# Experts' products as three fp16 products of high and low parts, with the experts' weights split during the projection stage

## The chip, the cores and the metric

One Trainium2 chip, one of its cores. The metric is the device time of one execution in microseconds (us), lower is better. TensorE, VectorE (DVE), ScalarE (ACT), GpSimd (POOL) and SyncE (SP) each work through their own instructions in order and wait for one another on semaphores. DMAs are issued from SP's, ScalarE's and GpSimd's queues.

## The reference

One layer of a streaming encoder over 4096 prompt tokens and 8 streams of 16 new tokens (33 tiles of 128 tokens), all in fp32:

```python
proj = rmsnorm(x) @ w_in                          # 1024 -> 3080 columns
out_a = rglru(causal_conv(x_lru)) * gelu(y_lru)   # a recurrence over time
o = gdn_sequence(q, k, v, g, beta)                # gated delta rule, chunks of 64 tokens
x = x + concatenate([out_a, norm(o) * silu(z)]) @ w_out
h = rmsnorm(x)
grp = argmax(h @ rg_w + rg_b)                     # 1 group of 4
top2 of the 8 experts of that group               # 32 experts in all
y = (silu(xblk @ w1[e]) * (xblk @ w3[e])) @ w2[e] # blocks of 128 tokens of one expert, 1024 -> 256 -> 1024
x = x + w_0 * y_0 + w_1 * y_1
return rmsnorm(x), states
```

## The kernel before, in words

Five stages follow one another, each a block with one program per engine.

**Projection** (`project_phase`). Nine groups of tokens: eight of 512 (`groups`, 0 to 7) and one of 128 (`stream=True`). A group is normed, transposed by TensorE (L279, T0 to T7, into four PSUM banks `turned`), and split into a high half `h_hi` by ScalarE (L355) and a low half `h_lo` by VectorE (L474), both fp16. Then 24 chunks of 128 output columns follow in the order of `sequence()`: Y and X (recurrence), Q (delta rule's q, k, v), Z (its gate). Each is 24 products of 512 columns in fp16: `w_hi h_hi`, `w_hi h_lo`, `w_lo h_hi` for eight slices of the inner width (L292). Three PSUM banks `pP` take turns; ScalarE empties them (L369, L376, L407), VectorE convolves the X and Q chunks (L496 to L505). G is the recurrence's gates (TensorE L301, ScalarE L382 to L386), R and O the recurrence and its store, S the silu of a convolved chunk (L400) and its store, N the squares for the next group's norm (L340) and the scaling of its rows, B the two small logits of the delta rule. In group 0 the weights `w_in` are loaded chunk by chunk into `stage` (two halves that take turns) and split: ScalarE makes `w_hi` (L348), VectorE `w_lo` (L467), and SP loads the next but one piece when `w_lo` is done (`w_split`, L221).

**Mixing** (`mix_phase`). 33 tiles; three of them are in work at a time, as X, Y and R steps of the list `MIX`, which fixes each engine's order. X builds the triangular inverse of the delta rule through a chain T, W, I, Z over TensorE, ScalarE and VectorE (L844, L854, L866, L1166); Y applies it and multiplies by `w_out`; R norms, routes and stores the normed rows `h2`. For the routing VectorE runs r0 and r1 on small operands; `h2` is made by GpSimd (step h2, L1087) and stored by ScalarE (step sh, L1037). `so` squares `ob` on ScalarE (L1025), `on` scales it on VectorE.

**Routing** (`routing_phase`). VectorE makes the tables of blocks; SP starts the loads of the first two experts.

**Experts** (`experts_phase`). 98 blocks of 128 rows, each of one expert, in the order of `EXPERTS`: `up` of block b+1 (L1539, eight fp32 products of 512 columns), `gT` of block b (L1547, two transposes), T0 and T1 of block b+2 (L1529, eight transposes), d0 and d1 of block b (L1557, four fp32 products of 512 columns). ScalarE does silu, gTc (copies the gated rows out of PSUM, L1578), T0c and d0c; VectorE does mul (L1606), T1c and d1c. GpSimd gathers the rows of a block. SP loads the weights of expert e+2 (3 MB, two DMAs, L1343) when the last block of expert e is done; `up` of the first block of e+2 waits for them (`ready`, which SP raises at L1489).

**Combine** (`combine_phase`). Gathers both experts' rows for each tile, adds, norms and stores.

What sets the order of the work around the change: `sequence()`, `MIX` and `EXPERTS`, and in the experts' stage the counts of blocks per expert.

## Time and profile before

| | us |
|---|---|
| median of 3 runs | 4444.15 |
| lowest and highest | 4443.91, 4451.27 |
| span of the profiled execution | 4435.0 |
| busy in it: TensorE, VectorE, ScalarE, GpSimd | 3787.8, 1902.0, 1410.0, 831.1 |

The profile is of one execution of the kernel. Its page gives busy time per engine, the span in 40 equal slices (a digit is the busy share in tenths; for the clock, tenths of full speed, and 9 is 90% or more), and the chain of work that ended last. That chain covers only the last 20 us here, so stages are read from stretches of the span and from the waits. In a line of the trace, "L292 MATMUL pP<-h_lo,w_hi" is a product of source line 292 that writes tile pP; "[1.93 <-SPq L1489]" says that the engine stood idle 1.93 us before it and that SP's queue at line 1489 released it. "x16" is a run of 16 such instructions, shown as one.

### The profile page before, as it was taken

What the parts mean: (1) busy time and instruction counts of PE and PEld (TensorE: products, weight loads), DVE (VectorE), ACT (ScalarE), POOL (GpSimd) and SP (SyncE); (2) the same over time, 40 slices, a digit from 0 to 9 for tenths busy, and PEclk for the clock granted to TensorE, in tenths of its full rate; (3) what the DMA queues carried; (4) which work ended last, traced back from release to release, by engine and by line L of the source; (5) the groups of instructions that cost most, each with busy time, mean ns of one, the idle gap of its engine ahead of it and who ended that gap; (6) DMA issues with size and microseconds to landing.
All of it is one profiled execution on the core that took longest, in us unless ns stands there. A gap on an engine that the chain in (4) does not pass through costs nothing. (4 is left out here: it accounts for less than half of the span.)

```text
span 4435.0 us, 64350 instructions
## 1 busy us (share of the span) xinstructions
PE 3787.8 (85%) x19068; PEld 2250.3 (51%) x19069; DVE 1902.0 (43%) x4556; ACT 1410.0 (32%) x2749; POOL 831.1 (19%) x853
## 2 busy tenths in 40 slices
PE   7999999999869989998988998839999999999600
PEld 3444444444556766666666666624444444444200
DVE  6456544564435565555555556441111111111255
ACT  6445544555423333333333333201111111111111
POOL 0000000000023333333333333201111111111133
PEclk9999999999979999999999999969999999999855
DMA  4211111111132112112111211023455455542387
GB/s 150 83 67 40 50 47 61 47 47 38 39 115 65 62 57 64 53 61 67 54 62 57 64 62 57 32 97 140 177 192 187 180 189 198 197 173 95 131 280 266
DMA packets 221780, 454.93 MB, mean 103 GB/s; under 512 B 20818, under 2 KB 132818, under 8 KB 213074
## 3 DMA queue, kind: packets, MB, share of 16 engines
q1 hardware_dynamic: 138498, 220.96, 14.8%
q10 hardware_dynamic: 54288, 146.56, 8.4%
q0 software_dynamic: 28864, 86.09, 6.0%
q14 instruction: 99, 0.81, 0.1%
q8 instruction: 31, 0.51, 0.0%
HBM read 303.84 MB, written 149.71 MB: 102 GB/s over the span
## 5 line engine op out<-in xcount | busy, mean ns | idle before, releaser
L1539 PE MATMUL ebank<-w,rowsT 128*128 x1568 | 708.0, 605 | 35.8 <-SPq L1489 32.5
L292 PE MATMUL pP<-h_hi,w_hi 128*128 128x512 f16 (+1 forms) x1728 | 623.7, 365 | 32.5 <-DVE h_lo L474 16.9
L292 PE MATMUL pP<-h_lo,w_hi 128*128 128x512 f16 (+1 forms) x1728 | 623.4, 365 | 0.0
L292 PE MATMUL pP<-h_hi,w_lo 128*128 128x512 f16 (+1 forms) x1728 | 623.2, 364 | 0.0
L1539 PEld LDWEIGHTS ebank<-w,rowsT 128*128 128x128 f32 x1568 | 302.8, 194 | 426.8 <-issue 426.8
L1557 PE MATMUL ebank<-w,guT 128*128 x784 | 353.4, 593 | 2.6 <-ACT guT L1578 2.6
L1606 DVE TENSOR_TENSOR gu<-ebank,sil 128x256 f32<-128x256 f32 x98 | 41.6, 425 | 703.8 <-ACT sil L1574 703.8
L505 DVE SCALAR_TENSOR_TENSOR cv<-win,cols_sb,cv 128x512 f32<-128x512 f32 (+1 forms) x432 | 305.3, 707 | 35.1 <-issue 3.6
L1574 ACT ACTIVATE sil<-ebank 128x256 f32<-128x256 f32 x98 | 37.7, 385 | 826.3 <-PE ebank L1539 826.3
L1166 DVE TENSOR_TENSOR WI<-bank,const 128x512 f32<-128x512 f32 x198 | 136.5, 689 | 376.6 <-PE bank L844 372.0
L292 PEld LDWEIGHTS pP<-h_hi,w_hi 128*128 128x128 f16 x1728 | 171.9, 100 | 220.9 <-issue 28.9
L1065 POOL TENSOR_TENSOR B<-G,const 128x512 f32<-128x512 f32 x198 | 256.2, 1313 | 143.7 <-DVE G L1147 138.8
L844 PEld LDWEIGHTS bank<-Tm,B 128*128 128x128 f32 x1584 | 195.0, 194 | 158.8 <-ACT Tm L995 78.5
L935 PE MATMUL bank<-w_out,mx 128*128 128x512 f32 x528 | 269.5, 594 | 0.8 <-DVE mx L1228 0.8
L844 PE MATMUL bank<-Tm,B 128*128 128x128 f32 x1584 | 228.0, 288 | 46.6 <-ACT Tm L991 42.7
L292 PEld LDWEIGHTS pP<-h_lo,w_hi 128*128 128x128 f16 x1728 | 172.0, 100 | 186.2 <-issue 11.2
L292 PEld LDWEIGHTS pP<-h_hi,w_lo 128*128 128x128 f16 x1728 | 172.1, 100 | 181.7 <-issue 0.8
L923 PE MATMUL bank<-w_out,ft 128*128 128x512 f32 x528 | 247.9, 593 | 0.0
L854 PEld LDWEIGHTS bank<-WI,Zm 128*128 128x128 f32 x1320 | 162.1, 193 | 142.9 <-ACT Zm L1003 71.8
L854 PE MATMUL bank<-WI,Zm 128*128 128x128 f32 x1320 | 192.5, 289 | 48.2 <-DVE WI L1166 34.3
L1557 PEld LDWEIGHTS ebank<-w,guT 128*128 128x128 f32 x784 | 140.9, 189 | 143.7 <-issue 143.7
L252 POOL TENSOR_TENSOR ss<-ss,eps 128x4 f32<-128x4 f32 (+1 forms) x9 | 1.8, 198 | 1111.2 <-ACT junk L340 1111.2
(282 smaller groups left out, 5691.6 us busy)
## 6 DMA issues: line engine op xcount, KB each, us to landing
w<-in_w SPq DMA_DIRECT2D x32, 2048.0 KB, 9.1
y<-yb ACTq DMA_DIRECT2D x98, 512.0 KB, 4.8
ft<-mixin SPq DMA_DIRECT2D x33, 1280.0 KB, 6.3
mixin<-qo ACTq DMA_DIRECT2D x128, 256.0 KB, 2.0
w<-in_w SPq DMA_DIRECT2D x32, 1024.0 KB, 12.5
xt<-in_x SPq DMA_DIRECT2D x33, 512.0 KB, 5.9
xr<-in_x SPq DMA_DIRECT2D x33, 512.0 KB, 4.7
x<-x2b ACTq DMA_DIRECT2D x33, 512.0 KB, 4.9
```

The source lines that it names most:

```text
L292: ins = nc.tensor.matmul(pP[n % NPB][:, 0:N], w[:, k, c0:c0 + P], h[:, k, 0:N], start=(k + i == 0), stop=(k == KD - 1 and i == 2))
L505: ins = nc.vector.scalar_tensor_tensor(dst, window(c, j, stream), cw(j), dst, ALU.mult, ALU.add)
L844: ins = nc.tensor.matmul(XB[:, h, :], Bs[s][:, h, :], Tm[:, h, :], start=True, stop=True)
L854: ins = nc.tensor.matmul(XC[:, h, :], Zm[:, h, :], WI[:, h, :], start=True, stop=True)
L923: ins = nc.tensor.matmul(flat((YD, YE)[half]), ft[p][:, QC + ZC + c, :], w_out[:, c, half * 512:half * 512 + 512], start=(c == 0), stop=False)
L935: nc.tensor.matmul(flat((YD, YE)[half]), mx[:, h, :], w_out[:, LC + h, half * 512:half * 512 + 512], start=False, stop=(h == H - 1)).then_ ...
L1065: nc.gpsimd.tensor_tensor(Bs[s][:, :, :], G[:, :, :], heads(mat(f"level{s}")), ALU.mult).then_inc(*did(n))
L1166: nc.vector.tensor_tensor(WI[:, :, :], XB[:, :, :], heads(mat("ident")), ALU.add).then_inc(*did(n))
L1539: ins = nc.tensor.matmul((M0, M1)[p][:, :], xT[p][:, k, :], w13[:, bass.ds(s, 1), k * 512:(k + 1) * 512].rearrange("p a n -> p (a n)"), st ...
L1557: ins = nc.tensor.matmul((OA, OB)[h][:, :], guT[p][:, k, :], w.rearrange("p a n -> p (a n)"), start=(k == 0), stop=(k == FE // P - 1))
L1574: nc.scalar.activation(sil[p][:, :], (M0, M1)[p][:, 0:FE], ACT.Silu).then_inc(*did(n))
L1606: nc.vector.tensor_tensor(gu[p][:, :], (M0, M1)[p][:, FE:2 * FE], sil[p][:, :], ALU.mult).then_inc(*did(n))
```

## The change

- The products `up` and `down` of the experts are each three fp16 products (high x high, high x low, low x high) in place of one fp32 product. The rows `h2` are stored as an fp16 high and low half (2 x 1024 columns, as many bytes as before) and transposed in fp16, 16 transposes in place of 8. The gated rows are split when they leave PSUM: ScalarE makes the high half (gTc), VectorE the low one (new step gTl).
- In the mixing stage ScalarE makes the high half of `h2` (new step hh) and VectorE the low half (new step hl); ScalarE's store (sh) waits for hl. GpSimd scales `ln2_row` once by 16.
- The experts' weights are 192 pieces of 128x1024 fp32. They are split into fp16 halves in groups 1 to 7 of the projection stage, 28 pieces in each of groups 1 to 6 and 24 in group 7: a step W follows each Y, X and Q chunk, two follow each Z chunk. SP loads a piece into `stage`, ScalarE makes its high half, VectorE (one W step later) the low half, and SP stores both to `ws` in HBM. Two buffers take turns. The experts' stage loads `ws` (one DMA an expert, 3 MB as before).
- Of the constant matrices only the identity is loaded in the first stage, the others at the start of the mixing stage.

```diff
-    return out + [("Z", 0), ("S", QC - 1), ("Z", 1), ("Z", 2), ("Z", 3)]
-
-
-def project_phase(nc, T, gb, const, cols):
+    out += [("Z", 0), ("S", QC - 1), ("Z", 1), ("Z", 2), ("Z", 3)]
+    paced, n = [], 0
+    for kind, m in out:
+        paced.append((kind, m))
+        if kind in "YXQZ":
+            for _ in range(2 if kind == "Z" else 1):
+                paced.append(("W", n))
+                n += 1
+    assert n == NW
+    return paced
...
+        halves = sb("halves", [P, 2, 2, WC], FP16)
...
+            def halved(g, j):
+
+                q = (g - 1) * NW + j
+                sp.wait_ge(expert_lo, q + 3)
+                sp.dma_start(T["ws"][bass.ds(q, 1)].rearrange("a p n -> p (a n)"),
+                             halves[:, j % 2, :, :].rearrange("p h n -> p (h n)")).then_inc(halves_out[j % 2], 16)
+
+            def experts(g):
+                n = steps_of(g)
+                for j in range(n):
+                    q = (g - 1) * NW + j
+                    sp.wait_ge(expert_lo, q + 1)
+                    sp.dma_start(stage[:, j % 2, :, :].rearrange("p k n -> p (k n)"),
+                                 T["we"][bass.ds(q, 1)].rearrange("a p n -> p (a n)")).then_inc(expert_in[j % 2], 16)
+                    if j:
+                        halved(g, j - 1)
+                halved(g, n - 1)
+
+            sp.wait_ge(w_split, len(wblocks))
+            with sp.Fori(1, groups - 1) as g:
+                load(g + 1, GT)
+                experts(g)
             load(groups, 1)
+            experts(groups - 1)
...
+                def expert_half(j):
+                    q = (g - 1) * NW + j
+                    act.wait_ge(expert_in[j % 2], ((g - 1) * (NW // 2) + j // 2 + 1) * 16)
+                    act.wait_ge(halves_out[j % 2], ((g - 1) * (NW // 2) + j // 2 + 1) * 16)
+                    nc.scalar.activation(halves[:, j % 2, 0, :], stage[:, j % 2, :, :].rearrange("p k n -> p (k n)"),
+                                         ACT.Copy, scale=W_SCALE).then_inc(expert_hi, 1)
...
+                    elif kind == "W":
+                        if not first and not stream and m < steps_of(g):
+                            expert_half(m)
...
+                def expert_rest(j):
+                    q = (g - 1) * NW + j
+                    dve.wait_ge(expert_hi, q + 1)
+                    nc.vector.scalar_tensor_tensor(halves[:, j % 2, 1, :], stage[:, j % 2, :, :].rearrange("p k n -> p (k n)"),
+                                                   W_SCALE, halves[:, j % 2, 0, :], ALU.mult, ALU.subtract
+                                                   ).then_inc(expert_lo, 1)
+
                 for kind, m in seq:
                     if first and block_of.get((kind, m), len(wblocks)) + 2 < len(wblocks):
                         split(block_of[kind, m] + 2)
                     if kind == "N" and following:
                         norm(g + 1, following)
+                    elif kind == "W":
+                        if not first and not stream and 0 < m <= steps_of(g):
+                            expert_rest(m - 1)
...
+                if not first and not stream and steps_of(g) == NW:
+                    expert_rest(NW - 1)
...
-R.lg.pe Y.so.act Y.ro.pool R.r0.dve R.sh.act
+R.lg.pe R.hh.act Y.so.act Y.ro.pool R.r0.dve R.hl.dve R.sh.act
...
+                elif n == "hh":
+                    act.wait_ge(h2_out, 16 * (t + 1))
+                    act.wait_ge(*at("h2", t))
+                    nc.scalar.activation(h2s[:, 0, :], h2b[:, :], ACT.Copy).then_inc(*did(n))
                 elif n == "sh":
-                    act.wait_ge(*at("h2", t))
-                    act.dma_start(T["h2"][bass.ts(t, P), :], h2b[:, :]).then_inc(h2_out, 16)
+                    act.wait_ge(*at("hl", t))
+                    act.dma_start(T["h2"][bass.ts(t, P), :], h2s[:, :, :].rearrange("p h n -> p (h n)")).then_inc(h2_out, 16)
...
-                    pool.wait_ge(h2_out, 16 * (t + 1))
+                    pool.wait_ge(*at("hl", t, 1))
...
+                elif n == "hl":
+                    dve.wait_ge(*at("hh", t))
+                    nc.vector.tensor_tensor(h2s[:, 1, :], h2b[:, :], h2s[:, 0, :], ALU.subtract).then_inc(*did(n))
...
-O.gT.pe O.gTc.act
+O.gT.pe O.gTc.act O.gTl.dve
...
-    w13, w2, loaded = weights
-    for dst, src in ((w13, "w13"), (w2, "w2")):
-        engine.dma_start(dst[:, p, :], T[src][bass.ds(e, 1)].rearrange("a p n -> p (a n)")).then_inc(loaded[p], 16)
+    ws, loaded = weights
+    engine.dma_start(ws[:, p, :, :], T["ws"][bass.ds(e * EC, EC)].rearrange("c p n -> p c n")).then_inc(loaded[p], 16)
...
-                    for k in range(4):
-                        c = 4 * h + k
-                        ins = nc.tensor.transpose(bank[:, k * P:(k + 1) * P], xb[p][:, c * P:(c + 1) * P], ident)
+                    for k in range(KD):
+                        ins = nc.tensor.transpose(bank[:, k * P:(k + 1) * P], xb[p][:, h, k * P:(k + 1) * P], ident16[:, :])
...
-                        ins = nc.tensor.matmul((M0, M1)[p][:, :], xT[p][:, k, :],
-                                               w13[:, bass.ds(s, 1), k * 512:(k + 1) * 512].rearrange("p a n -> p (a n)"),
-                                               start=(k == 0), stop=(k == KD - 1))
+                        for i, (x, w) in enumerate(PARTS):
+                            ins = nc.tensor.matmul((M0, M1)[p][:, :], xT[p][:, x, k, :], half(s, k // 2, w, k % 2 * 512),
+                                                   start=(k + i == 0), stop=(k == KD - 1 and i == 2))
...
-                    pe.wait_ge(*at("gTc", b))
+                    pe.wait_ge(*at("gTl", b))
                     for k in range(FE // P):
-                        w = w2[:, bass.ds(pe_slot[0], 1), k * D + h * 512:k * D + h * 512 + 512]
-                        ins = nc.tensor.matmul((OA, OB)[h][:, :], guT[p][:, k, :], w.rearrange("p a n -> p (a n)"),
-                                               start=(k == 0), stop=(k == FE // P - 1))
+                        for i, (x, w) in enumerate(PARTS):
+                            ins = nc.tensor.matmul((OA, OB)[h][:, :], guT[p][:, x, k, :],
+                                                   half(pe_slot[0], W13 // WC + k, w, h * 512),
+                                                   start=(k + i == 0), stop=(k == FE // P - 1 and i == 2))
...
+                elif n == "gTl":
+                    dve.wait_ge(*at("d1", b, 2))
+                    dve.wait_ge(*at("gTc", b))
+                    nc.vector.tensor_tensor(guT[p][:, 1, :, :].rearrange("p k n -> p (k n)"), GB[:, 0:FE],
+                                            guT[p][:, 0, :, :].rearrange("p k n -> p (k n)"), ALU.subtract).then_inc(*did(n))
```

## Rows read from the trace of the kernel before

**Rows 1.** Page, 40 slices: TensorE's busy tenths, and its granted clock.

```profile
PE   7999999999869989998988998839999999999600
...
PEclk9999999999979999999999999969999999999855
```

**Rows 2.** Tile xt, three groups: loads by SP, and time to landing.

```profile
L202 SPq DMA_DIRECT2D xt<-in_x x12: 332/333/333, 460.9 to 749.0; - x12
...
DMA to landing us min/median/max: 3.1/5.1/6.6
```

**Rows 3.** Stretches of a group: length, busy us by engine, clock, DMA.

```profile
485.50:530.30 44.80, 43.43 (x190) 19.45 (x188) 30.60 (x52) 36.62 (x44) 0.00 (x0) 1.00 0.06 23
530.30:583.30 53.00, 53.00 (x332) 25.30 (x330) 34.84 (x71) 23.41 (x37) 1.21 (x2) 1.00 0.15 54
583.30:598.00 14.70, 14.70 (x70) 6.69 (x69) 0.00 (x0) 1.84 (x4) 0.00 (x0) 1.00 0.19 71
```

**Rows 4.** One experts block in time: start us, us, engine, line, op.

```profile
3404.99 7.03 PE L1539 MATMUL ebank<-w,rowsT 128*128 x16
...
3411.86 0.38 PE L1547 MATMUL ebank<-const,gu 128*128 128x128 f32 x2
...
3412.08 1.04 PE L1529 MATMUL ebank<-const,rows 128*128 128x128 f32 x8
...
3412.47 0.42 DVE L1606 TENSOR_TENSOR gu<-ebank,sil 128x256 f32<-128x256 f32 x1 [6.59 <-ACT sil L1574]
...
3412.95 3.61 PE L1557 MATMUL ebank<-w,guT 128*128 x8
```

**Rows 5.** Experts: waits (us, times, longest); one load; TensorE behind it.

```profile
PE ebank L1539 <- SPq L1489: 32.5, 15, 2.4
...
3607.81 0.85 SPq L1343 DMA_DIRECT2D w<-in_w  x2
...
3621.01 8.82 PE L1539 MATMUL ebank<-w,rowsT 128*128 x16 [1.99 <-SPq L1489]
```

**Rows 6.** Mixing stage, one tile in time.

```profile
1704.38 0.40 ACT L1025 ACTIVATE junk<-ob,sc 128x128 f32<-128x128 f32 x1 [5.41 <-DVE ob L1221]
...
1710.15 0.68 DVE L1166 TENSOR_TENSOR WI<-bank,const 128x512 f32<-128x512 f32 x1
...
1710.88 1.16 PE L854 MATMUL bank<-WI,Zm 128*128 128x128 f32 x8 [0.51 <-DVE WI L1166]
```

**Rows 7.** Projection, TensorE in time: two products in a row.

```profile
500.06 0.38 PE L292 MATMUL pP<-h_lo,w_hi 128*128 128x512 f16 x1
500.28 0.38 PE L292 MATMUL pP<-h_hi,w_lo 128*128 128x512 f16 x1
```

**Rows 8.** First group in time: a low part, load, high part.

```profile
106.45 1.22 DVE L467 SCALAR_TENSOR_TENSOR w_lo<-stage,w_hi 128x1024 f16<-128x1024 f32 x1
...
107.69 0.54 SPq L221 DMA_DIRECT2D stage<-in_w_in  x1
...
111.98 1.06 ACT L348 ACTIVATE w_hi<-stage 128x1024 f16<-128x1024 f32 x1 [0.45 <-DMA stage<-in_w_in]
```

**Rows 9.** DMA issues: a 512 KB store, median us to landing.

```profile
h<-h2b ACTq DMA_DIRECT2D x33, 512.0 KB, 2.6
```

**Rows 10.** Projection in time: evacuation, silu, convolution, square, B step.

```profile
538.79 0.60 ACT L376 ACTIVATE win<-pP 128x512 f32<-128x512 f32 x1 [2.02 <-PE pP L292]
539.44 0.63 ACT L400 ACTIVATE qo<-cv 128x512 f32<-128x512 f32 x1
...
539.51 0.17 DVE L496 COPY win<-carry 128x3 f32<-128x3 f32 x1
...
540.39 2.40 DVE L505 SCALAR_TENSOR_TENSOR cv<-win,cols_sb,cv 128x512 f32<-128x512 f32 x3
...
551.16 1.06 ACT L340 ACTIVATE junk<-xt 128x1024 f32<-128x1024 f32 x1 [0.90 <-issue]
...
574.78 0.18 DVE L546 SCALAR_TENSOR_TENSOR amax<-asum,alog 128x16 f32<-128x16 f32 x1 [4.86 <-ACT alog L420]
```

More of the change, by code:

```diff
@@ L44 @@
 PROJ = 1.0 / (W_SCALE * H_SCALE)
+G_SCALE = 4.0
+WC = 1024
 W13, W2 = KD * 2 * FE, (FE // P) * D
+DOWN = 1.0 / (W_SCALE * G_SCALE)
+EC = (W13 + W2) // WC
+NW = 28
 COLS = {}
@@ L193, in project_phase @@
         table_out = sem("table_out")
+        expert_in = [sem(f"expert_in{n}") for n in range(2)]
+        expert_hi = sem("expert_hi")
+        expert_lo = sem("expert_lo")
+        halves_out = [sem(f"halves_out{n}") for n in range(2)]
+        NC = NE * EC
+        steps_of = lambda g: NW if not isinstance(g, int) or g < groups - 1 else NC - NW * (groups - 2)
         block = ctx.enter_context(nc.Block())
@@ L221, in _ @@
                 sp.dma_start(stage[:, n % 2, :, 0:w], T["w_in"][:, :, c:c + w]).then_inc(weights_in[n % 2], 16)
-            with sp.Fori(2, groups) as g:
-                load(g, GT)
+            def halved(g, j):
[17 more added lines that the diff above has]
+                experts(g)
             load(groups, 1)
+            experts(groups - 1)
+            for p in range(2):
+                sp.wait_ge(halves_out[p], 16 + NC // 2 * 16)
             sp.wait_ge(zeroed, 1)
@@ L456, in _ @@
                 dve.sem_inc(s, 16)
+            dve.sem_inc(expert_lo, 2)
             def norm(g, nt):
@@ L1487, in arrived @@
             def arrived(e, p):
-                sp.wait_ge(loaded[p], (e - p) * 16 + 32)
+                sp.wait_ge(loaded[p], (e - p) * 8 + 16)
                 sp.sem_inc(ready, 1)
@@ L1544, in step @@
                     pe.wait_ge(*at("gTc", b, 1))
+                    pe.wait_ge(*at("gTl", b, 1))
                     pe.wait_ge(*at("mul", b))
```

76 lines of the change are left out of this document (44 added, 32 removed).

## The prediction

> **What bounds the kernel now.** I read the 40 slices first, then busy times by stage, then the waits, and last single stretches in order of time. The slices show three stages in which TensorE is busy (projection to about 1180 us, mixing to about 2940, experts to about 4170) and a tail without it [rows 1]. In the projection one group of 512 tokens takes 143.2 us (the first loads of x in three groups' views run from 460.9 to 749.0; less the 1.6 us that the four loads of a group are apart, this is two groups), and TensorE is busy in nearly all of it [rows 2, 3]. The reader should see where the others have room: in the stretch with the gates ScalarE is busy 36.6 of 44.8 us, in the next 23.4 of 53.0, and VectorE does nothing in the last 14.7 us of a group [rows 3]. In the experts' stage one block takes 11.40 us and TensorE never pauses inside it; fifteen times it waits some 2.2 us for weights [rows 4, 5]. In the mixing stage TensorE waits once a tile for a chain that passes through VectorE [rows 6].
>
> **Experts' stage.** A block's up products are eight fp32 products of two passes each, 16 in the 6.87 us between 3404.99 and 3411.86, 0.43 each; an fp16 product of 512 columns starts every 0.216 us in the projection [rows 4, 7]. Up: 16 x 0.43 = 6.87 becomes 24 x 0.216 = 5.18. Down: 8 x 0.43 = 3.44 becomes 12 x 0.216 = 2.59. The 8 transposes took 0.87 (3412.08 to 3412.95); 16 in fp16 of 128 columns at a quarter of 0.216 take 0.86. The two of the gated rows stay at 0.22 [rows 4]. Before: 6.87 + 0.22 + 0.87 + 3.44 = 11.40; after: 8.86. A wait is added: the down product now needs a VectorE subtraction (gTl) behind ScalarE's copy. On VectorE it queues behind the product of the next block's gate, which ends at 3412.89; gTl, like that product 0.42, ends at 3413.31 and the down product starts at about 3413.33, where its turn is 3412.95 [rows 4]: 0.38 us, so 9.24 us a block. Behind gTl VectorE queues only the second transposed copy, which has the 2.59 us of the down product as cover. 98 x (11.40 - 9.24) = 212 us gained.
>
> Against this stand the weight loads. They start when the last block of expert e is done and are needed by e+2, so an expert with two blocks covers one block's time. A load issued at 3607.81 let TensorE go at 3621.01, 13.2 us later, and others lie up to 13.7 [rows 5]. Bytes are the same (3 MB), so I keep 13.5: the stall grows from 2.2 to 13.5 - 9.24 = 4.3 us, 15 times: 64 instead of 32.5. Some of these stalls cost more: 16 passes take 8.82 us behind this one and 7.03 undisturbed, 1.8 us more, as behind 10 of the 15 [rows 4, 5]. It is the granted clock, which stands at 9 tenths and more in all slices but those of the stages' joints and the tail, where TensorE has stood [rows 1]; it falls from 2.4 to 1.2 GHz for a while. With 4.3 us idle I count all 15: 27 instead of 18. Together +40. **Stage: -172** (bounds -150, if loads slow to 15 us beside denser traffic, and -190, if gTl is hidden).
>
> **Projection stage: the new ring.** 192 pieces of weight (128x1024) are split in groups 1 to 7, 28 a group (24 in the last). Each costs ScalarE 1.05 us and VectorE 1.22, as the splits of the first group do [rows 8]. As busy time it fits. But the pieces go through two buffers, and each turn is a ring over four queues: VectorE's low part of piece j ends, SP stores j and loads j+2 behind it, ScalarE makes the high part of j+2 (waiting in order, the evacuations of PSUM queued behind), and VectorE makes the low part one slot later, behind the next chunk's convolution. I call D the time from the end of a low part to the start of the high part two pieces on. In the first group, without the store, D is 4.3 us: the low part ends at 107.67, the load goes at 107.69, the high part starts at 111.98 [rows 8]. Here the load's runs are 4 KB: such a load lands in 3.1 us when alone, and the four in a row take 6.4 to 6.6 for the last, issued 1.6 us after the first, so 1.5 apart [rows 2]. The store of 512 KB (a like one lands in 2.6 [rows 9]) is issued 0.54 before. If the load merely follows by issue, D = 0.54 + 3.1 + 0.2 = 3.8; if it also waits for the store's packets, 2.6 + 1.5 + 0.1 = 4.2. I take 4.2, and up to 5.1 where stores of the convolution's output cut in (0.5 MB per two slots).
>
> A Trainium skill rule bears on this D. DMA: Bandwidth & Descriptors, "Two DMAs through the same engine are not ordered", says descriptors of one queue start in order but are pipelined, with reads and writes in separate queues; by it the load needn't wait for the store's writes, D would be 3.8 and the sum below 29 us less. No row here has a store directly before a load on SP's queue.
>
> In the slots of the convolution two slots make one ring: D 4.2 + high 1.05 + silu and its store issue 1.2 + evacuation of the next chunk 0.65 + convolution 3.3 + low 1.22 + hand-overs 0.2 = 11.8 us, where TensorE needs 2 x 24 x 0.216 = 10.36 [rows 7, 8, 10]. In the four Z chunks, with two pieces each, a ring is 4.2 + 1.05 + 1.22 + 0.1 = 6.6 against 5.18. So the ring, not TensorE, sets the pace. I walked one group in queue order with these durations (the same walk gives 145.2 us for the group of before, which took 143.2). From the last transpose on:
> - To the end of Q2's evacuation: 70.0 before, 79.8 after. ScalarE had 8 us idle in the gates' stretch [rows 3] and gets some 9 high parts plus ring waits.
> - To Z0's evacuation: 55.2 before; five rings are 59, and the next group's squares (four of 1.06 with small reads behind them, 4.9 on ScalarE) and the B step, for which VectorE waits 4.9, hold two rings longer [rows 10]: 72.3 after.
> - To the next group's first low half: 17.4 before; four rings of 6.6 less the part already under way: 27.5 after.
>
> TensorE has three PSUM banks, so it runs ahead of ScalarE by at most three chunks, finishes Z3 and then stands some 20 us, because ScalarE turns to the next group's h_hi only behind its last high part. 182.0 - 145.2 = 37 us a group, six groups, and 14 for the last, which has no pieces in its last two chunks: **+235** (D 3.8: +206; D 5.1: +301). After a pause of that length the clock falls as above; 1.7 us a group and little else, since the other pauses are ScalarE's anyway: +13 (0 to +35). **Stage: +248.**
>
> **Mixing stage.** Per tile ScalarE gets hh (1.05) and VectorE hl (1.22, two sources in SBUF, going on from 0.42 at 256 columns and 0.69 at 512, as WI's, by 0.53 for 512 more [rows 4, 6]). hh falls where ScalarE had stood 5.4 us before the squares of ob (1704.38), and h2 is long there: nothing; without that cover it would cost 1.05 a tile. hl stands ahead of r1, on and I2 in VectorE's queue. There VectorE works without a gap until WI at 1710.15, and TensorE waits 0.5 us for it at 1710.88 [rows 6]. So hl goes on the path whole: 33 x 1.22 = **+41** (0 to +60). The store of h2 now waits for hl in ScalarE's queue and holds the first Tm a little; that is covered, since its product meets VectorE's delay anyway. POOL's h2 waits for hl instead of the store: no cost.
>
> **Small edits.** The constant matrices (896 KB, 2.6 us at 1.5 us per 512 KB [rows 2]) are loaded at the mixing stage's start instead of the kernel's, all but one, and POOL scales one row there before it begins. What the start gains the joint loses; for the scaling **+2**, bounds -3 and +8. One DMA in place of two per expert, and the half-width junk: nothing, for they lie behind waits that stay.
>
> **Sum.** -172 + 248 + 41 + 2 = +119. The profiled execution's span is 4435.0, the median 4444.15; the 9.1 us around it stay. 4444 + 119 = **4563 us**.
>
> **Rivals.**
> - *The pieces are hidden.* If D comes out so short or ScalarE so early that the ring stays under 10.36 us, which needs D below 2.8, only their busy time in the gates' stretch is left: the walk gives +4.9 a group, +35. Then 4444 - 172 + 35 + 41 + 2 = 4350, faster. It decides from D = 2.8 down. Against it: even the first group's load alone takes 4.3. For it: by busy time alone there is room on both engines [rows 3].
> - *The ring is slower.* Stores and loads at 1 MB a piece with the output stores beside them push D to 5.1, clock drops cost 30: 301 + 30 + 41 + 2 - 160 = +214, 4658.
> - *The mixing stage takes nothing*, as other waits absorb hl: 4522; inside the forecast's own range.
> - *The fp16 products don't run at 0.216 in this stage*: then the gain shrinks, 4650 or so; nothing supports it but that the loads and gathers are denser.
>
> **How the numbers follow.** Forecast 0.70 (4465 to 4640), hidden pieces 0.14, slower ring or dearer products 0.16. The range is 4465 (D 3.8, mixing 0, experts -190, no clock cost) to 4680 (slower ring): 0.82. About 0.2% (9 us) is what a measurement can tell from no change. Faster 0.14 (the hidden pieces), within 0.2% 0.03 (a ring halfway, D near 3), slower 0.83.
>
> **What would show it.** In the changed profile: groups 1 to 6 about 180 us apart, ScalarE waiting for the DMA into stage, VectorE's h_lo late, and TensorE idle some 20 us before its transposes' second half; mixing tiles 1.2 us longer; blocks of 9.24 us, and fifteen waits of 4 us for weights. Groups of 150 us or less would refute the ring; blocks over 9.5 or a stage over 1010 us the experts' term.

## The result, and the profile after

The changed kernel takes **4858.14 us** (median of 4 runs, 4853.62 to 4866.4) where the kernel before takes 4444.53 (4443.91 to 4451.27): ratio **1.093**, 95% interval 1.0915 to 1.0946. The sign of the forecast was right, the size was not: 4563 us was forecast, and 4858 lies outside its range of 4465 to 4680. The profiled execution's span is 4864.8 us (4435.0 before).

The page of the changed kernel, in 40 slices: TensorE's busy tenths and its granted clock, which answer to [rows 1].

```profile
PE   8878686686867688888888888888489897888600
...
PEclk9989898898988799999999999998699998999855
```

The projection stage now shows sixes and sevens where [rows 1] had nines, and there the clock falls to 8 and 7. The stages' lengths, read from the first and last squares of the mixing stage (tile sqb) and the first and last down products, say where the time went:

| us | before | after | difference | forecast |
|---|---|---|---|---|
| projection, to the first sqb | 1256.6 | 1628.3 | +371.7 | +248 |
| mixing, first to last sqb | 1540.2 | 1679.5 | +139.3 | +41 |
| experts, first to last down product | 1154.9 | 1060.2 | -94.7 | -172 |
| joints and tail | | | +13.5 | +2 |

**Projection.** Loads of x of two groups, five groups apart (start, us, engine, line, tiles), as in [rows 2]:

```profile
173.54 1.96 SPq L221 DMA_DIRECT2D xt<-in_x  x4
...
1172.13 1.98 SPq L221 DMA_DIRECT2D xt<-in_x  x4
```

That is 199.7 us a group ((1172.13 - 173.54) / 5), 143.2 before: six groups make some 336 us of the stage's 372. From the load of x of the 128 tokens (1370.1) to the first sqb it is 258 us, 223 before: 35 more. Two stretches of one group (columns as in [rows 3]):

```profile
690.00:751.00 61.00, 40.69 (x247) 19.03 (x244) 29.66 (x47) 26.68 (x39) 1.21 (x2) 0.83 0.60 207
751.00:772.00 21.00, 3.67 (x16) 3.27 (x16) 9.39 (x11) 9.37 (x13) 0.00 (x0) 0.50 0.63 226
```

In the last 21 us TensorE is busy for 3.7 (at a granted clock of 0.50), VectorE and ScalarE for 9.4 each: nobody is full, all turn round the ring of the pieces. One turn of it (VectorE's low parts, SyncE's stores and loads, ScalarE's high parts, from three answers in order of time by engine):

```profile
1124.81 1.22 DVE L535 SCALAR_TENSOR_TENSOR halves<-stage,halves 128x1024 f16<-128x1024 f32 x1
```

```profile
1126.22 0.35 SPq L246 DMA_DIRECT2D ws<-halves  x1
1126.85 0.33 SPq L254 DMA_DIRECT2D stage<-in_we  x1
```

```profile
1130.86 1.06 ACT L405 ACTIVATE halves<-stage 128x1024 f16<-128x1024 f32 x1 [5.54 <-DMA stage<-in_we]
...
1135.91 1.06 ACT L405 ACTIVATE halves<-stage 128x1024 f16<-128x1024 f32 x1 [2.15 <-DMA stage<-in_we]
```

The low part ends at 1126.03, the high part two pieces on starts at 1130.86: D is 4.8 us, and 5.5 in the next turn (1130.36 to 1135.91). The page's groups of instructions and of DMA issues (KB each, median us to landing) say that this is the rule:

```profile
L405 ACT ACTIVATE halves<-stage 128x1024 f16<-128x1024 f32 x192 | 202.5, 1055 | 486.8 <-DMA stage<-in_we 485.3
...
stage<-in_we SPq DMA_DIRECT2D x192, 512.0 KB, 4.6
ws<-halves SPq DMA_DIRECT2D x192, 512.0 KB, 3.0
```

ScalarE waits 485 us for loads of pieces. The median load lands in 4.6 us; 3.1 is the fastest of the twelve loads of x in [rows 2], on which D was built. From the low part's end: 0.19 to the store, 0.63 to the load, 4.6 to its landing, 0.1 to ScalarE: D is 5.5. Taken piece by piece from the trace, its median is 5.5 too, and its mean higher (6.7), since ScalarE comes late to some pieces between two groups.

**Waits of TensorE** (us in total, times, longest). L1577 answers to L1489 of [rows 5]; the last line, idle time put down to no engine, has no counterpart there.

```profile
PE pT L322 <- DVE h_lo L528: 177.9, 9, 28.5
PE bank L924 <- DVE WI L1242: 113.4, 32, 3.7
...
PE ebank L1625 <- SPq L1577: 63.3, 15, 4.7
...
PE ebank L1625 <- issue: 44.8, 81, 0.8
```

**Mixing.** The chain of [rows 6] in a tile of the changed kernel, VectorE first, then GpSimd and TensorE:

```profile
2215.30 1.22 DVE L1325 TENSOR_TENSOR h2s<-h2b,h2s 128x1024 f16<-128x1024 f32 x1
...
2218.06 2.78 DVE L1347 SCALAR_TENSOR_TENSOR esel<-lg,goh,esel 128x8 f32<-128x8 f32 x3
...
2222.05 1.76 DVE L1301 TENSOR_TENSOR onb<-ob,ro 128x512 f32<-128x512 f32 x1
2223.73 0.68 DVE L1242 TENSOR_TENSOR WI<-bank,const 128x512 f32<-128x512 f32 x1
```

```profile
2218.33 1.27 POOL L1139 TENSOR_TENSOR B<-G,const 128x512 f32<-128x512 f32 x1
2219.55 1.26 POOL L1133 TENSOR_TENSOR AT<-AT,const 128x512 f32<-128x512 f32 x1
2220.78 5.37 POOL L1139 TENSOR_TENSOR B<-G,const 128x512 f32<-128x512 f32 x4
```

```profile
2224.46 1.75 PE L924 MATMUL bank<-WI,Zm 128*128 128x128 f32 x8 [3.66 <-DVE WI L1242]
2226.01 3.00 PE L993 MATMUL bank<-w_out,ft 128*128 128x512 f32 x4
```

hl takes the 1.22 us forecast. But the three products on esel, 8 columns wide, take 2.78 us together; before they took 0.86. They now lie beside GpSimd's products, and onb takes 1.76. WI, one of whose inputs is in PSUM, lies beside them too and takes the 0.68 of [rows 6]. TensorE waits 3.66 us, not 0.51, and then eight products take 1.75 instead of the 1.16 of [rows 6], since the granted clock is lower: over the two runs of products above it is 0.62 of full speed in the mean (its two levels are 1.2 and 2.4 GHz), and it was 1.00 over the same two runs of the kernel before (columns as in [rows 3]):

```profile
2224.46:2229.01 4.55, 4.55 (x14) 2.86 (x15) 0.00 (x0) 0.60 (x1) 1.69 (x2) 0.62 0.00 0
```

```profile
1710.88:1713.76 2.88, 2.88 (x14) 1.88 (x15) 0.00 (x0) 0.60 (x1) 2.88 (x4) 1.00 0.00 0
```

The kernel before already had such a meeting, of an instruction one column wide with GpSimd's mask (the like one takes 0.15 us in the changed kernel, at 2221.98):

```profile
1708.39 1.24 DVE L1276 TENSOR_TENSOR dif<-m8e 128x1 f32<-128x1 f32 x1
1709.55 0.68 DVE L1225 TENSOR_TENSOR onb<-ob,ro 128x512 f32<-128x512 f32 x1
```

```profile
1708.29 1.31 POOL L1065 TENSOR_TENSOR B<-G,const 128x512 f32<-128x512 f32 x1
```

**Experts.** One block, as in [rows 4]:

```profile
3618.97 5.35 PE L1625 MATMUL ebank<-ws_sb,rowsT 128*128 x24 [0.39 <-issue]
...
3624.37 1.06 PE L1614 MATMUL tbank<-ident,rows 128*128 128x128 f16 x16
3625.69 2.76 PE L1643 MATMUL ebank<-ws_sb,guT 128*128 x12 [0.26 <-DVE guT L1699]
3629.18 1.03 PE L1625 MATMUL ebank<-ws_sb,rowsT 128*128 x4 [0.73 <-issue]
```

The up product's 24 passes take 5.35 with the last one's end, as summed. From the first transpose to the down product it is 1.32 us, the low part's wait of 0.26 in it, where 0.86 + 0.38 = 1.24 were forecast. New is the idle time before `up`, 0.39 and 0.73 us in turns, put down to no engine. Ahead of it the end of the last pass shows as well: twelve passes that start 0.216 apart end after 2.76 us, not 2.59. A block takes 10.05 us (the second `up` behind this one starts at 3639.06, two blocks on), not 9.24.

### The profile page after: what moved, and what is told of

The parts are those of the page before. It is cut to its first block and busy times, and to the rows that moved or that the text cites. A ratio compares the mean times of both kernels' runs of the same rounds, so it can differ in the third digit from the quotient of the medians.

```text
span 4864.8 us, 72087 instructions
## 1 busy us (share of the span) xinstructions
PE 3730.5 (77%) x21028; PEld 2233.9 (46%) x21029; DVE 2249.8 (46%) x4880; ACT 1676.8 (34%) x2974; POOL 831.2 (17%) x854
## 5 line engine op out<-in xcount | busy, mean ns | idle before, releaser
L335 PE MATMUL pP<-h_hi,w_hi 128*128 128x512 f16 (+1 forms) x1728 | 642.8, 376 | 98.9 <-ACT win L429 73.3
L1625 PE MATMUL ebank<-ws_sb,rowsT 128*128 x2352 | 560.1, 398 | 111.4 <-SPq L1577 63.3
L1625 PEld LDWEIGHTS ebank<-ws_sb,rowsT 128*128 128x128 f16 x2352 | 237.9, 101 | 433.1 <-issue 204.0
L405 ACT ACTIVATE halves<-stage 128x1024 f16<-128x1024 f32 x192 | 202.5, 1055 | 486.8 <-DMA stage<-in_we 485.3
L1694 DVE SCALAR_TENSOR_TENSOR gu<-ebank,sil 128x256 f32<-128x256 f32 x98 | 41.6, 425 | 644.6 <-ACT sil L1662 644.6
L924 PE MATMUL bank<-WI,Zm 128*128 128x128 f32 x1320 | 216.5, 314 | 127.3 <-DVE WI L1242 113.4
L535 DVE SCALAR_TENSOR_TENSOR halves<-stage,halves 128x1024 f16<-128x1024 f32 x192 | 233.8, 1221 | 162.5 <-ACT halves L405 162.5
L1643 PE MATMUL ebank<-ws_sb,guT 128*128 x1176 | 272.3, 381 | 28.5 <-DVE guT L1699 28.5
L993 PE MATMUL bank<-w_out,ft 128*128 128x512 f32 x528 | 291.0, 681 | 0.0
L924 PEld LDWEIGHTS bank<-WI,Zm 128*128 128x128 f32 x1320 | 182.9, 214 | 222.1 <-DVE WI L1242 150.4
L914 PE MATMUL bank<-Tm,B 128*128 128x128 f32 x1584 | 229.3, 289 | 59.5 <-ACT Tm L1061 55.6
```

What stands on the lines that cost most here:

```text
L335: ins = nc.tensor.matmul(pP[n % NPB][:, 0:N], w[:, k, c0:c0 + P], h[:, k, 0:N], start=(k + i == 0), stop=(k == KD - 1 and i == 2))
L405: nc.scalar.activation(halves[:, j % 2, 0, :], stage[:, j % 2, :, :].rearrange("p k n -> p (k n)"), ACT.Copy, scale=W_SCALE).then_inc(expe ...
L535: nc.vector.scalar_tensor_tensor(halves[:, j % 2, 1, :], stage[:, j % 2, :, :].rearrange("p k n -> p (k n)"), W_SCALE, halves[:, j % 2, 0, ...
L914: ins = nc.tensor.matmul(XB[:, h, :], Bs[s][:, h, :], Tm[:, h, :], start=True, stop=True)
L924: ins = nc.tensor.matmul(XC[:, h, :], Zm[:, h, :], WI[:, h, :], start=True, stop=True)
L993: ins = nc.tensor.matmul(flat((YD, YE)[half]), ft[p][:, QC + ZC + c, :], w_out[:, c, half * 512:half * 512 + 512], start=(c == 0), stop=False)
```

## The experiments

Each kernel below is compared by stage with the changed kernel. All but the last two were timed once, beside the kernel before on the same chip (4448 to 4457 there); the changed kernel's own four times span 13 us, so differences of that size say nothing. Stage lengths in us, from the profile of one execution each; the experts' stage comes out between 1056 and 1060 us in the kernels that don't touch it:

| run | time | projection | mixing | experts |
|---|---|---|---|---|
| changed kernel | 4858 | 1628 | 1680 | 1060 |
| e1_no_pieces | 4491 | 1256 | 1686 | 1056 |
| e2_low_same_slot | 4649 | 1428 | 1672 | 1057 |
| e3_gpsimd_waits | 4675 | 1626 | 1508 | 1056 |
| e4_registers_ahead | 4894 | 1625 | 1675 | 1096 |
| e5_reads_inside | 4855 | 1626 | 1679 | 1054 |
| e6_hl_later | 4710 | 1619 | 1539 | 1057 |
| e7_before_waits (kernel before) | 4411 | 1261 | 1497 | 1155 |
| e8_stores_elsewhere | 4913 | 1699 | 1675 | 1056 |
| e9_no_stores | 4741 | 1518 | 1680 | 1057 |
| e10_paced_anew | 4580 | 1368 | 1677 | 1056 |
| e11_one_read | 4823 | 1630 | 1673 | 1022 |
| e12_mixing_both | 4650 | 1623 | 1474 | 1057 |
| e13_all_cures | 4343 | 1367 | 1466 | 1016 |
| e14_before_waits_timed (kernel before) | 4410 | 1260 | 1496 | 1159 |

**The ring of the projection: e1, e2, e8, e9, e10.**

```diff
-        steps_of = lambda g: NW if not isinstance(g, int) or g < groups - 1 else NC - NW * (groups - 2)
+        steps_of = lambda g: 0
...
```

> The changed kernel without the pieces: nothing of the experts' weights is loaded, split or stored in the projection stage (so the fp16 parts of the weights are left out; the experts load the same number of bytes of other fp16 data in their place). Mixing and experts' stages are as in the changed kernel. Theory A (the projection's loss is the ring of the pieces alone, 56 us a group): groups go back to 143 us, the stage loses its +372, time 4858 - 372 = 4486, and the mixing stage stays at 1679 us, the experts' stage at 1062. Rival B (part of the loss is the moved constants and the fp16 junk, or a clock that stays low): groups stay above 150 us and the time above 4530.

The stage is back at 1256 us. Its whole loss comes from the pieces, none from the moved constants, and the mixing stage's loss isn't theirs.

```diff
-                        if not first and not stream and 0 < m <= steps_of(g):
-                            expert_rest(m - 1)
+                        if not first and not stream and m < steps_of(g):
+                            expert_rest(m)
...
```

> VectorE makes the low part of piece j in the slot of piece j itself, right behind the convolution that now lies beside ScalarE's high part, and no longer one slot later. All work stays. Ring theory: the ring of two slots loses silu and store issue 1.2, the evacuation 0.65 and the convolution 3.3 and is left with D 5.2 + 1.05 + 1.22 + 0.2 = 7.7 us, below TensorE's 10.36, so that only the four Z slots with two pieces each (7.7 against 5.18) and the gates' stretch still hold; my walk in queue order gives 168 to 174 us a group instead of 200: stage -190 (-170 to -220), time about 4670. Rival (the stores and loads take DMA or memory bandwidth from the rest, or ScalarE's added busy time is what costs): the order of the low parts changes little, groups stay above 190 us, time above 4790.

Groups are 170.8 us apart and the stage is 200 us shorter, with the same bytes and the same work on each engine: it is the ring's length that costs, not bandwidth or ScalarE's work.

For the size of D, two runs: the stores on another queue, and no stores.

```diff
...
-                sp.dma_start(T["ws"][bass.ds(q, 1)].rearrange("a p n -> p (a n)"),
+                pool.dma_start(T["ws"][bass.ds(q, 1)].rearrange("a p n -> p (a n)"),
...
```

> The changed kernel with the stores of the split pieces issued by GpSimd on its own queue and no longer by SyncE; order of the low parts as in the changed kernel. Theory (a load of a piece lands in 4.6 us, not 3.1, because a store of 512 KB stands directly ahead of it on the same queue): the load lands in 3.1 to 3.5 us, D falls from about 5.2 to 4, groups from 200 to 188 or so, time about 4770. Rival (the load is slow because the DMA engines are shared with that store and the stores of the outputs, whichever queue they come from): the load still lands in 4.3 us or more and groups stay within 5 us of 200; GpSimd's issue may even add to it, 4850 to 4900.

```diff
-                    if j:
-                        halved(g, j - 1)
-                halved(g, n - 1)
...
-                    act.wait_ge(halves_out[j % 2], ((g - 1) * (NW // 2) + j // 2 + 1) * 16)
+                    act.wait_ge(expert_lo, q + 1)
...
```

> The changed kernel without the stores of the split pieces (loads, high and low parts stay, in the changed kernel's order; the fp16 weights don't reach DRAM, the experts load the same bytes of other fp16 data). This takes away what shares the DMA engines with the loads of pieces. Theory (the load lands in 4.6 us because 512 KB of store are on the DMA engines with it): it lands in 3.1 to 3.5 us, D is 3.5 to 3.9, and the walk gives 173 to 176 us a group: time about 4858 - 170 = 4690. Rival (the load is slow by itself in this stage, beside the stores of the convolution's outputs): it lands in 4.2 us or more, groups above 185 us, time above 4760.

DMA issues of both pages (KB each, median us to landing), first with GpSimd's stores, then without stores:

```profile
ws<-halves POOLq DMA_DIRECT2D x194, 512.0 KB, 5.0
stage<-in_we SPq DMA_DIRECT2D x192, 512.0 KB, 4.1
```

```profile
stage<-in_we SPq DMA_DIRECT2D x192, 512.0 KB, 3.6
```

Behind a store on the same queue a load lands in 4.6 us, beside one from another queue in 4.1, with none in 3.6. So 1.0 us comes from the store, half of it left when only the queue is another; my theory of the queue's order holds for half at most, and both runs fell between what the two theories expected. That a store from another queue still slows the load agrees with what the Trainium skill says (DMA: Bandwidth & Descriptors, "Issuing engines are not separate DMA queues"): transfers of all queues share the same DMA engines. The other 0.5 us above the 3.1 of [rows 2] is there without any store of pieces. When GpSimd issues the stores they land in 5.0 us, later than the loads, and it is for them that ScalarE now waits:

```profile
ACT halves L419 <- DMA ws<-halves: 552.4, 151, 13.1
```

So the ring got longer, groups of 209 us, and that run's time says nothing on the load. Without stores a group takes 184 us, where my walk gave 173 to 176 for loads of 3.1 to 3.5.

```diff
-        if kind in "YXQZ":
-            for _ in range(2 if kind == "Z" else 1):
-                paced.append(("W", n))
-                n += 1
+        for _ in range(PIECES.get((kind, m), 0)):
+            paced.append(("W", n))
+            n += 1
...
```

> Low part in the same slot, as in the run of that name, and the 28 pieces of a group put at other places of the sequence (fewer in X and early Q slots, some behind S, G, R, O, N and B steps), as a search over my walk in queue order found best. If the walk is a fair account of the stage, groups take 160 us instead of 170: time 4649 - 65 = 4585 (4560 to 4620). Rival (the walk leaves out what counts, e.g. the sharing of DMA engines): no gain over 4649, or a loss.

4580 against 4585 expected, groups of 161.9 against 160. The walk that gave 182 us a group in the prediction met both runs that change the order of the work (e2, e10) once D was taken from the changed kernel's trace (5.2, as put down for e2), and is thus a fair model of the stage; what was wrong in the prediction was D. Loads land in 5.0 us in this run, though, and in 4.4 in e2: even with a store ahead there is no one figure.

**The mixing stage: e3, e6, e7, e12.**

```diff
-Y.outA2.pe X.B4.pool
+Y.outA2.pe R.pw.pool X.B4.pool
...
+                elif n == "pw":
+                    pool.wait_ge(*at("r1", t))
+                    pool.sem_inc(*did(n))
```

> In the mixing stage GpSimd holds its fourth-level mask product (B4), and AT's behind it, until VectorE is through r1 of the routing; the subtraction hl stays where it is. Theory (VectorE's small products on esel are slow, 2.78 us for three instead of 0.86, because GpSimd's tensor_tensor runs beside them): they go back to 0.86, WI comes about 1.9 us earlier, TensorE's wait of 3.66 falls to about 1.7 and part of its clock comes back: mixing stage -60 to -100 us, time 4760 to 4800. Rival (the VectorE operations are slow for another reason, or the queue is only longer by hl): esel stays at 2.8, no gain, or GpSimd's later work costs something: 4850 to 4880.

The stage loses 172 us, more than I expected, and is shorter than that of the kernel before though hl is still in VectorE's queue. The groups of VectorE's instructions (busy, mean ns | idle) of the changed kernel and of this one:

```profile
L1347 DVE SCALAR_TENSOR_TENSOR esel<-lg,goh,esel 128x8 f32<-128x8 f32 x99 | 81.6, 824 | 7.7 <-issue 0.3
...
L1301 DVE TENSOR_TENSOR onb<-ob,ro 128x512 f32<-128x512 f32 x33 | 55.9, 1693 | 3.6 <-POOL ro L1151 3.6
...
L1354 DVE TENSOR_SCALAR dif<-gpad,m 128x4 f32<-128x4 f32 x33 | 23.7, 718 | 0.0
```

```profile
L1304 DVE TENSOR_TENSOR onb<-ob,ro 128x512 f32<-128x512 f32 x33 | 22.8, 692 | 3.6 <-POOL ro L1151 3.6
...
L1350 DVE SCALAR_TENSOR_TENSOR esel<-lg,goh,esel 128x8 f32<-128x8 f32 x99 | 22.4, 226 | 9.4 <-issue 3.1
...
L1357 DVE TENSOR_SCALAR dif<-gpad,m 128x4 f32<-128x4 f32 x33 | 7.0, 213 | 0.0
```

I had counted esel alone (1.8 us a tile). onb (1.0) and dif (0.5) are stretched too: 3.3 us a tile in all. Not all of that is new: in the kernel before onb took 1.26 us in the mean and the two instructions on dif 1.32 together, which is 0.87 in the changed kernel. What hl's place added is 1.8 in esel and 0.4 in onb less 0.45 in dif, some 1.8 us a tile beside its own 1.22. With GpSimd's wait TensorE's wait for WI falls from 113.4 to 4.9 us. The stage's 172 us are 5.2 a tile. Most of the rest is TensorE's clock, which doesn't fall any more there (granted 1.00 from 2216.57 to 2219.44, against the 0.62 above):

```profile
2216.57 1.16 PE L924 MATMUL bank<-WI,Zm 128*128 128x128 f32 x8 [0.24 <-DVE WI L1245]
2217.56 1.88 PE L993 MATMUL bank<-w_out,ft 128*128 128x512 f32 x4
```

The two runs of products took 1.75 and 3.00 us in the changed kernel: 1.7 us a tile. WI itself, with one operand in PSUM, takes 690 ns in both kernels.

```diff
-R.lg.pe R.hh.act Y.so.act Y.ro.pool R.r0.dve R.hl.dve R.sh.act
+R.lg.pe R.hh.act Y.so.act Y.ro.pool R.r0.dve
...
-X.W8.pe X.Z4.pe X.Z4c.act X.I8.dve R.r3.dve Y.outB2.pe
-X.T8.pe X.T8c.act Y.outB3.pe X.B64.pool
+X.W8.pe X.Z4.pe X.Z4c.act X.I8.dve R.r3.dve R.hl.dve Y.outB2.pe
+X.T8.pe X.T8c.act R.sh.act Y.outB3.pe X.B64.pool
```

> In the mixing stage the subtraction hl and the store of h behind it move from ahead of r1 to behind r3, into VectorE's idle time later in the tile; nothing else changes and GpSimd doesn't wait. Theory (hl costs 1.22 us on the path and pushes VectorE's small products into the time in which GpSimd multiplies; both go when it is moved): mixing stage back to 1540 to 1550, time about 4720. Rival (the fp16 parts' 512 KB store or ScalarE's hh are what slows the stage, not hl's place): mixing stays above 1640, time above 4820.

As expected, 1539 us, the length of the kernel before. So the place of hl and of the store behind it is worth the whole loss. The lengths are equal, the waits are not: TensorE waits 60.9 us for WI (34.3 before), with onb still beside GpSimd's products at 1.69 us in the mean (1.26 before), and less for Tm (30.7 for 42.7) and for xn (10.8 for 26.3). That the fp16 copy and the store cost nothing holds only within these shifts of 12 to 27 us.

```diff
                     pool.wait_ge(*at(f"W{s}", t, 1))
+                    if s == 4:
+                        pool.wait_ge(*at("r1", t, 2))
```

> The kernel before, all of it, with one wait more: GpSimd holds B4 (and AT's mask behind it) until VectorE is through r1 of the routing of the tile two back. Theory: beside GpSimd's products the kernel before loses 1.0 us in dif (1.24 against 0.21) and 0.6 in onb (1.26 against 0.69) a tile, of which TensorE's wait for WI shows 0.51 a tile; the mixing stage gets shorter by 0.3 to 0.9 us a tile, 10 to 30 us, time about 4425. Rival (GpSimd's masks become late and TensorE waits for them, or the effect exists only with hl in the queue): no change or up to 20 us longer.

> In the mixing stage hl and the store of h behind r3 and, besides, GpSimd holding B4 until r1 of the tile two back is done. Theory (the two losses, hl on the path and GpSimd beside VectorE's small products, overlap, as each cure alone took 148 and 183 us): what is left is the stage of the kernel before with its own contention cured, 1497 us: time 4858 - 183 = 4675, no more than 15 us below the run with the wait alone. Rival (they add up): mixing at 1450 us or less, time below 4640.

The kernel before has the same loss: with the wait its mixing stage takes 1497 us, 44 less, a little more than I expected. The two cures together (e12, the edits of e6 and e7) give 1474, less than the 1497 that I took for the floor; the rival's 1450 isn't reached either. Part of the difference lies in a wait that I had called covered:

```profile
PE bank L914 <- ACT Tm L1061: 55.6, 33, 1.8
```

```profile
PE bank L914 <- ACT Tm L1061: 30.7, 33, 1.1
```

The first is the changed kernel, the second the run with both (42.7 in the kernel before, 43.0 in e7). The store of h stands ahead of the first copy of Tm in ScalarE's queue, and TensorE waits for that copy. These 12 us, against e7, are half of the 22; TensorE's wait for xn is 16 shorter (26.7 to 10.9). It is 10.8 in the changed kernel too but 27.4 in e1, and no run here isolates the reason.

**The gap ahead of `up`: e4, e5, e11.**

```diff
-                    e = pe.value_load(tabs["expert"][0:1, bass.ds(b, 1)], min_val=0, max_val=NE - 1)
-                    s = pe.value_load(tabs["slot"][0:1, bass.ds(b, 1)], min_val=0, max_val=1)
+                    e, s = ahead.pop()
...
                         pe_slot[0] = pe.value_load(tabs["slot"][0:1, bass.ds(b, 1)], min_val=0, max_val=1)
+                        if coming[0] is not None:
+                            look(coming[0])
...
```

> TensorE's own queue reads the expert's number and slot of the next block before it waits for the down product of the block before, instead of right ahead of the up product, and its loop turns behind an up product. No product changes. Theory (the 0.39 and 0.73 us ahead of each up product that the profile calls issue are TensorE's own register reads, which fp32 passes of 0.43 us used to hide): both gaps go to under 0.1, a block takes about 9.5 us instead of 10.05, experts' stage -50 us (98 x 0.5), time about 4806. Rival (the gap is the waits for the copies or the weights' first load, not the registers): the gap stays, time 4858.

```profile
3663.39 2.76 PE L1644 MATMUL ebank<-ws_sb,guT 128*128 x12 [1.30 <-issue]
3665.99 5.34 PE L1624 MATMUL ebank<-ws_sb,rowsT 128*128 x24
```

The gap ahead of `up` is gone, so the register reads do make it; but it came back as 1.30 us ahead of the down product, where the three reads now follow short transposes; two reads more there made 1.04 us more than the 0.26 before. The stage got 35 us longer. The part of the theory that failed is that TensorE's queue could read while it waits there: it reaches the reads only when the transposes are nearly through.

```diff
                     for k in range(FE // P):
+                        if k == 1 and coming["up"] is not None:
+                            read(*(("expert", "expert") if h == 0 else ("slot", "slot")), coming["up"])
...
```

> As in the run that read the registers ahead, but each read (expert's number, slot) stands between long products: the next up product's two reads after the first three passes of each down product's half, every other down product's read in the middle of an up product. Theory (TensorE's queue needs some 0.5 us for each read and runs ahead of the engine by a few instructions only, which is 1 us or more of passes of 0.216 but next to nothing of transposes of 0.06): the gaps of 0.39 and 0.73 ahead of the up products vanish and those of 1.3 ahead of the down products go back to the 0.26 that VectorE's low part costs; a block takes 9.5 us, stage -55 us, time about 4803. Rival (a read stops the engine wherever it stands): each read shows as a gap inside a product, a block stays at 10 us or above, time 4850 to 4900.

```profile
3662.58 0.82 PE L1648 MATMUL ebank<-ws_sb,guT 128*128 x3 [0.26 <-DVE guT L1737]
3663.58 2.28 PE L1648 MATMUL ebank<-ws_sb,guT 128*128 x9 [0.17 <-issue]
3665.70 5.34 PE L1626 MATMUL ebank<-ws_sb,rowsT 128*128 x24
```

A read behind three passes of 0.216 shows as a gap again, and the down product takes 3.1 us from start to start, not 2.6. The read in the middle of the 24 passes costs nothing (5.35 with it, 5.34 without). A block takes 9.83 us. The time, 4855 us, is the changed kernel's and not the 4803 of the theory; the stage is 6 us shorter, where 0.2 us a block would make 20, and no run shows where the rest went.

```diff
-                    s = pe.value_load(tabs["slot"][0:1, bass.ds(b, 1)], min_val=0, max_val=1)
+                    s = e % 2
```

> In the experts' stage TensorE reads only the expert's number ahead of an up product and takes the slot from it by register arithmetic (number modulo 2) instead of a second read from SBUF. Theory (each read costs TensorE's queue 0.4 to 0.5 us and the twelve short passes before it hide about 0.5): the gaps of 0.39 and 0.73 fall to 0 and 0.3; a block 9.65 instead of 10.05, stage -35 us, time about 4820. Rival (register arithmetic costs as much as a read, or the wait for the weights is what costs): gaps as before, 4850 to 4860.

```profile
3628.35 2.76 PE L1643 MATMUL ebank<-ws_sb,guT 128*128 x12 [0.26 <-DVE guT L1699]
3630.95 5.34 PE L1625 MATMUL ebank<-ws_sb,rowsT 128*128 x24
...
3637.66 2.76 PE L1643 MATMUL ebank<-ws_sb,guT 128*128 x12 [0.26 <-DVE guT L1699]
3640.51 4.70 PE L1625 MATMUL ebank<-ws_sb,rowsT 128*128 x21
```

4823 against 4820 expected. From down to up it is 2.60 us now, which is twelve passes and no gap, and 2.85 where the loop turns; before it was 3.15 and 3.49. The reads cost some 0.5 us each and a run of twelve passes hides one of them. That the time was met so closely is in part luck: blocks take 9.31 and 9.56 us in turns, less than the 9.65 expected, and the wait for the weights grew from 63.3 to 74.3 us, since a shorter block covers less of the load.

**All together: e13, e14.**

> The changed kernel with the four cures that each gained alone: low part in the same slot and pieces placed anew (4580 where the changed kernel takes 4858), hl behind r3 and GpSimd's wait (4650), one register read ahead of the up product (4823). The three stages are apart in time, so the gains should add: 4858 - 278 - 208 - 35 = 4337 us (4325 to 4360), ratio to the kernel before 0.976. Rival (stages share something, e.g. the clock or DRAM traffic that moves from one to the other): a sum that falls short by 30 us or more, 4370 or above.

> The kernel before with GpSimd's wait alone, timed in rounds beside the run with all cures: if the 46 us of the single look hold, 4403 us or so, ratio 0.990, and the run with all cures is another 65 us faster, which is then what the fp16 products themselves are worth once their costs are hidden. Rival (the single look was a lucky one): within 10 us of the kernel before.

Both were timed five times. All cures: **4342.68 us** (4328.32 to 4362.47), ratio to the kernel before **0.978** (0.9756 to 0.9797). The kernel before with GpSimd's wait: **4409.52 us** (4404.09 to 4413.96), ratio 0.992 (0.9902 to 0.9929). The gains add to within 6 us, so nothing that the stages share shows. Against the kernel before with the same wait the run with all cures is 67 us faster, but that is not the worth of the fp16 products alone: by stage it is +107 in the projection, -31 in the mixing stage and -144 in the experts' stage. The 31 come from the moved store and the shorter wait for xn (e12), and whether the kernel before would gain from a later store too was not tried.

## Why the prediction was wrong, point by point

- **Projection, +248 forecast, +372 measured. The mechanism was right, the term D was mis-sized.** The ring sets the pace (e1, e2, e10); ScalarE waits for the load, TensorE stands at the group's end (28.5 us at most where 20 were forecast). D is 5.5 us, not 4.2. I built D from the fastest load of x [rows 2], 3.1 us, although the median of those twelve is 5.1, and although the load of [rows 8], with no store ahead, lands 4.2 us after its issue (4.5 in the median of all loads of that tile in the page of before). The upper bound that I gave, 5.1, was below the typical value. By the prediction's own sums (+235 at 4.2, +301 at 5.1) a D of 5.5 gives some +330, an estimate; of the 42 us left over, some 20 lie in the last groups (35 where 14 were forecast), and the clock was to cost 13.
- **The rule weighed against D** (the Trainium skill, DMA: Bandwidth & Descriptors, "Two DMAs through the same engine are not ordered") would have made D 3.8. e9 shows that a store ahead does cost the load 1.0 us (4.6 against 3.6), so it was right not to follow it, and wrong to stop at 0.4 more.
- **Mixing, +41 forecast, +139 measured.** The 1.22 us of hl and its place on the path were right. The step that failed is the term "hl goes on the path whole: 33 x 1.22", which leaves the other instructions of VectorE their times and TensorE its clock. The later start moved esel beside GpSimd's masks, and TensorE's wait for WI grew from 34.3 to 113.4 us, 79 more. Behind that longer wait the granted clock falls, for which the prediction had a term in the other two stages and none in this one: the products of L924, L993 and L1000 are busy for 533 us in all where the same ones took 460 before, 73 more. The row that showed the danger was in the trace of before: dif, one column wide, took 1.24 us there at 1708.39, just as GpSimd began at 1708.29. The Trainium skill states it (SBUF — State Buffer, "Who interferes with whom"): a VectorE instruction with two SBUF inputs and a GpSimd one that reads SBUF exclude each other. The runs agree: esel (0.82 for 0.23) and onb (1.69 for 0.69) are slow beside GpSimd, WI with an operand in PSUM is not (0.69 in both). I hadn't weighed that rule.
- **The store in ScalarE's queue** was called covered. It isn't quite: TensorE's wait for Tm went from 42.7 to 55.6 us, 0.4 a tile.
- **Experts, -172 forecast, -95 measured.** Right were the pass of 0.216 and the weights' wait (63.3 us, 15 times, for 64); the transposes and gTl together came within 0.08 us. The step that failed is the block's sum, 9.24 us, which has no term for TensorE's own register reads, since TensorE never pauses between blocks in the row of before: passes of 0.43 us hid two reads, passes of 0.216 don't. Idle times of 0.39 and 0.73 us, 0.56 in the mean, the 0.17 of the last pass's end that shows ahead of them and the 0.08 are the 0.81 us that a block is longer than forecast, 79 us in 98 blocks; the sign that I had named (blocks over 9.5, a stage over 1010) came. e11 gives 38 us of the stage back.
- **Rivals.** The slower ring (4658) was the right one, and still 200 us short, since the other two stages missed in the same direction. The chance of 0.16 that I gave it, and the range's end at 4680, took the errors of those stages as small; both come from instructions whose cost I read as hidden because next to no wait showed in the trace of before.

What stays open: whether the output stores or something else makes the 0.5 us between a load of 3.1 and one of 3.6; no run took the output stores away.

## What to carry to other kernels

A ring through DMA and several queues is priced by the landing time of that very transfer under that traffic; if the ring is longer than the work of one turn, shortening it pays though no engine gets less to do (the low part in the same slot: -210 us). When an instruction is put ahead of others on VectorE, look at what GpSimd does at the time to which they move. And when passes get shorter, the instructions between them, such as register reads, come into the open: no gap in the old trace is no proof that there is none.

## What the runs showed of the hardware

- VectorE's products on 8 columns with their tensors in SBUF (esel) take 0.23 us with GpSimd held back (e3) and 0.82 in the mean beside GpSimd's tensor_tensor of 128x512; one of 512 columns (onb) takes 0.69 and 1.69 so. With an operand in PSUM (WI) it stays at 0.69.
- A register read from SBUF on TensorE's queue costs about 0.5 us (e4, e11); twelve fp16 passes of 512 columns ahead of it hide one (e11), and so does the middle of a run of 24, with no trace (e5); behind three passes 0.35 us of it shows (1.00 us from start to start for passes of 0.65, e5).
- 512 KB loads of pieces land, in the median, in 3.6 us without stores of the same size beside them (e9), in 4.1 with stores from another queue (e8), in 4.6 directly behind a store on the same queue, and there in 4.4 to 5.0 as the order of the work changes (e2, e10).
- TensorE's granted clock is 0.62 over the 4.55 us behind an idle time of 3.66 us, and 1.00 behind idle times of 0.51 (kernel before) and 0.24 us (e3) at the same place.
